# One output product of the mixing stage issued inside the attention units, and the down products' wait on block sums issued later

## Chip, cores, metric

The kernel runs on one core of one Trainium2 chip. The metric is the device time of one execution in microseconds (us). All data is fp32.

## The reference

The reference is two blocks over 256 tokens of width 1024. The first has a retention group, an RWKV group and sixteen experts. The second has two layers of mixing and feed-forward, and the change lies there:

```
for layer in range(DEPTH_2):                       # 2 layers
    h = rmsnorm(x, norm_mix[layer])
    z = h @ w_in[layer]
    ...
    o_a = nsa_mixer(...)      # 4 heads: compressed, selected and window attention, gated
    o_b = diff_mixer(...)     # 4 heads, difference of two softmaxes
    o_c = mlstm_mixer(...)    # 4 heads
    o_d = dilated_mixer(...)  # 4 heads
    x = x + jnp.concatenate([o_a, o_b, o_c, o_d], axis=-1) @ w_out[layer]
    h = rmsnorm(x, norm_ffn[layer])
    x = x + (jax.nn.silu(h @ w_gate[layer]) * (h @ w_up[layer])) @ w_down[layer]
return rmsnorm(x, norm_final)
```

## The kernel before, in words

TensorE (PE), ScalarE (ACT), VectorE (DVE) and the DMA queue on SyncE (SP) each run one straight program written out by hand. Semaphores order them: an instruction with waits holds everything behind it on its engine. Weights of 2 MB per slot stream through a ring in SBUF, in a fixed order; `W.take` waits for the landing of the next slot, and a count on `W.used` lets SP load the slot that has been left. PSUM has eight banks of 128 x 512 fp32.

**Mixing** (function `mixing`). Tokens lie in two tiles `t` of 128. The width 1024 of the concatenated mixers falls into four groups `g` of 256: 0 is `o_a`, 1 `o_b`, 2 `o_c`, 3 `o_d`. The attention runs as `NU` = 14 units `u`, one mixer part and token tile each; the last are 10 and 11 (mlstm), 12 and 13 (dilated, token tile 0 and 1). For each unit PE does

- `score(u + 1)` (dilated units: L2268) into banks 0 and 1,
- `turn(u)` (L2282), transposes of the probabilities into banks 2 and 3, which waits for DVE's `weigh(u)` (for the dilated units L2536) and so for ACT's exponentials (L2386),
- projection work and other items that fill the gaps (`fills`, `halved`); at the last two units nothing is left,
- `values(u)` (L2303) into bank 4 or 5, which waits for ACT's copy of the transposes (`keep`, L2404).

The item `o0` (L2231) transposes group 0 of the attention output at the end of unit 11. It is kept to `mixT` by ACT (L2373). Items such as `o0` take bank 6 or 7, in turns worked out in `banks`; `held` says whose copy must be over first.

After the units PE takes the two weight slots of `w_out` and runs, in this order: `o3`, `out_product(0, 0)`, `out_product(0, 1)`, `out_product(3, 0)`, `o1`, `o2`, `out_product(3, 1)`, and the four products of groups 1 and 2. `out_product(g, t)` (L2334) is four matmuls of 512 columns, 128 x 128 weights, which the profile shows as eight records, two each. Banks 0 and 1 collect token tile 0, banks 2 and 3 token tile 1. `o3` waits for DVE's output of unit 13 (L2559). `o1` and `o2` wait for `o_ready`: that is the end of a chain of norms on DVE (L2653 to L2671) with one square root on ACT (L2454). On ACT the copies of `o3`, `o1` and `o2` are queued behind that square root. Then DVE adds the banks to `x` (L2678), and the feed-forward begins with its norm.

**Feed-forward** (function `feed_forward`). The products use a seven-product scheme (Strassen's, in Winograd's form) for 2 x 2 blocks; the weight-side sums are made by DVE (`block_sum`, L2936, four per weight slot, counted on `sums_ready`). Twelve units of gate and up (L2750) are followed by the down product (L2821): for each `j` from 0 to 7, products `m1` to `m7`, one matmul (two records) each. `m1` to `m3` read the weights as they landed, `m4` to `m7` read block sums. At each even `j`:

```
w = W.take(pe)
pe.wait_ge(sums_ready, 4 * (UNITS + j // 2) + 4)
```

so all seven wait until the fourth block sum of the slot is made. At `j` = 0, `m1` also waits for the gates (ACT, L2876) and `m4` for DVE's last copy out of the units (L2974). The last three `j` are run product by product, behind a wait for all block sums (L2846).

Of the kernel before, what the change touches and what calls it, by code (L numbers as in the profile page):

```python
# [12 lines left out]
P = 128  # L13
# [2011 lines left out]
def mixing(nc, K, layer):  # L2025

    A, W = K.A, K.W
# [55 lines left out]
    by = lambda name: "dve" if name in turns or name in ("f", "qk0", "qk1") else "act"  # L2083
    ordinal = [sum(by(other) == by(name) for other in items[:n + 1]) for n, name in enumerate(items)]
    banks, held, turn_of = [], [], {6: -1, 7: -1}
    for n, name in enumerate(items):
        mine = (6, 7) if name[:2] == "qk" else ((6,) if turn_of[6] <= turn_of[7] else (7,))
        banks.append(mine)
        held.append([turn_of[b] for b in mine if turn_of[b] >= 0])
        for b in mine:  # L2090
            turn_of[b] = n

    keys = lambda u: 16 if units[u][0] == "cmp" else P * (units[u][1] + 1)
    maps = lambda u: 2 if units[u][0] == "diff" else 4
    scale = {"cmp": HD ** -0.5, "slc": HD ** -0.5, "win": HD ** -0.5, "dil": HD ** -0.5, "diff": 32 ** -0.5}
# [39 lines left out]
    def tensor(pe):  # L2135
# [150 lines left out]
        def values(u):  # L2286
# [16 lines left out]
                    last = nc.tensor.matmul(out, probsT[:, u % 2, (t + 1) * j + k, :], v, start=(k == 0), stop=(k == t))  # L2303
            last.then_inc(pv_made, 1)

        turn_input(0, 1)
        pe.wait_ge(t_scaled, 1)
        pe.wait_ge(t_kept, 1)
# [4 lines left out]
        for u in range(NU):  # L2313
            if u + 1 < NU:
                score(u + 1)
            if u in leads:
                item(leads[u])
            if u in halved:
                half_job(halved[u], 0)
            turn(u)  # L2320
            if u in halved:
                half_job(halved[u], 1)
            for name in fills[u]:
                item(name)
            values(u)
        ws = [W.take(pe) for _ in range(2)]
        pe.wait_ge(scores_kept, NU)
        pe.wait_ge(pt_kept, NU)

        def out_product(g, t):  # L2330
            kept(f"o{g}")
            for k in range(2 * g, 2 * g + 2):
                for n in range(2):
                    last = nc.tensor.matmul(K.ps[:, 2 * t + n, :], K.mixT[:, k, P * t:P * t + P], ws[n][:, k, :],  # L2334
                                            start=(g == 0 and k == 0), stop=(g == 2 and k == 5))
                    if g == 0 and t == 0 and k == 0 and n == 0:
                        last.then_inc(W.used, 1)
            if g == 2:
                last.then_inc(out_made, 1)

        item("o3")
        out_product(0, 0)
        out_product(0, 1)
        out_product(3, 0)
        item("o1")
# [112 lines left out]
    def vector(dve, meanwhile):  # L2458
# [216 lines left out]
        meanwhile(dve)  # L2675
        for t in range(TT):
            dve.wait_ge(out_made, t + 1)
            nc.vector.tensor_tensor(K.x[:, t, :], K.x[:, t, :], K.ps[:, 2 * t:2 * t + 2, :].rearrange("p a b -> p (a b)"),  # L2678
                                    ALU.add).then_inc(x_ready, 1)

    A.high = top
# [3 lines left out]
def feed_forward(nc, K, layer):  # L2685
# [49 lines left out]
    def tensor(pe):  # L2735
# [91 lines left out]
        for j in range(TAIL):  # L2827
            if j % 2 == 0:
                w = W.take(pe)
                pe.wait_ge(sums_ready, 4 * (UNITS + j // 2) + 4)  # L2830
            if j == 0:
                pe.wait_ge(gate_opened, FCH)
                pe.wait_ge(took, 5 * (UNITS - 1))
            for n in range(1, 8):
                if j == 0 and n == 4:
                    pe.wait_ge(hid_opened, FCH)
                    pe.wait_ge(took, 5 * UNITS)
                if j % 2 == 0 and n == 3:
                    pe.wait_ge(hid_summed, FCH * layer + j // 2 + 1)
                last = down(j, f"m{n}", w)  # L2840
                if j % 2 == 0 and n == 1:
                    last.then_inc(W.used, 1)
                elif j % 2 == 1 and n == 7:
                    last.then_inc(made, 1)
# [453 lines left out]
```

## Time and profile before

| | |
|---|---|
| median of 3 runs | 2016.33 us (2011.97 to 2017.17) |
| the profiled execution, its own time | 2017.03 us |
| its span in the trace | 2015.2 us |
| PE busy | 1690.9 us, 84% |
| DVE busy | 700.5 us, 35% |
| ACT busy | 355.9 us, 18% |
| mean granted TensorE clock | 0.909 of full speed |
| load of a 2 MB slot of `w_out`, issue to landing | 7.7 us |

Time outside the span is 1.8 us. "Idle before" is the time in which an engine had nothing running ahead of an instruction, with the instruction whose end let it go. A row of the timeline merges instructions of one line. PEclk (clock) is the share of full speed granted to TensorE: 1.00 is 2.4 GHz, 0.50 is 1.2 GHz. The first mixing layer of the second block spans about 1163 to 1361 us, the first feed-forward layer 1363 to 1585, the second mixing layer 1585 to 1784, the second feed-forward layer the rest.

### The profile page before, as it was taken

The page shows a single profiled execution, that of the slowest core. Times are in us where ns is not written, and L with a number is a line of the kernel's source. Part 1 is how long each engine was busy: PE and PEld are TensorE (multiplying, and loading weights), DVE is VectorE, ACT ScalarE, POOL GpSimd, SP SyncE. Part 2 cuts the span into 40 slices and gives each one's busy share as a digit, 9 for nine tenths or more (in the row PEclk, how much of TensorE's full clock was granted, in tenths as well). Part 3 has the DMA queues.
Part 4 walks back from the last instruction along what each step waited for, and adds up shares of the span by engine and source line. Part 5 has one row for each costly group of instructions (what it writes and reads, how often), then busy time and mean ns, then how long its engine had stood idle before and what let it go on. Part 6 is the DMA issues. An engine that isn't in the chain of part 4 may idle for free.

```text
span 2015.2 us, 31978 instructions
## 1 busy us (share of the span) xinstructions
PE 1690.9 (84%) x14184; PEld 1151.5 (57%) x14184; DVE 700.5 (35%) x1247; ACT 355.9 (18%) x827; POOL 91.0 (5%) x94
## 2 busy tenths in 40 slices
PE   6999898987989675655655689988999999899997
PEld 3665458957975431211211257758994476669963
DVE  2005373363332300000000124555664244536663
ACT  2010122342231220000000122421010124310000
POOL 0000003402311000000000000000000000000000
PEclk9999898987999788877877889989999899899999
DMA  9521111040024599999999952214454522225440
GB/s 373 198 90 78 67 42 44 4 168 2 4 73 162 209 406 428 427 428 427 429 427 428 428 187 84 84 42 171 170 204 167 217 88 84 84 84 209 168 178 21
DMA packets 35593, 382.08 MB, mean 190 GB/s; under 512 B 6977, under 2 KB 10433, under 8 KB 12673
## 3 DMA queue, kind: packets, MB, share of 16 engines
q1 hardware_dynamic: 35458, 380.04, 47.2%
q8 instruction: 113, 1.85, 0.4%
q14 instruction: 22, 0.18, 0.0%
HBM read 378.98 MB, written 1.05 MB: 189 GB/s over the span
## 4 chain that ended last, share of the span: by engine, by line
PE 50%; DMA 11%; DVE 3%; ACT 1%; issue 1%; SPq 0%; DVEq 0%; ACTq 0%
PE psum L2750 14%; PE psum L1873 7%; PE psum L2821 7%; DMA arena<-in_w_moe 6%; PE psum L2162 6%; DMA weight_ring<-in_w_moe 5%; PE psum L2165 3%; PE psum L2334 3%; PE psum L1848 3%; PE psum L2303 1%; PE psum L1828 1%; PE psum L2282 1%; PE psum L2268 1%; PE psum L2191 1%; PE psum L1898 0%
## 5 line engine op out<-in xcount | busy, mean ns | idle before, releaser
L1873 PE MATMUL psum<-weight_ring,arena 128*32 128x512 f32 x640 | 142.6, 721 | 127.7 <-DMA arena<-in_w_moe 93.5
L1269 PE MATMUL psum<-arena 64*64 64x64 f32 x4608 | 150.8, 223 | 19.6 <-PEq L962 8.8
L2750 PE MATMUL psum<-arena 128*128 128x128 f32 x1408 | 165.2, 275 | 1.7 <-DVE arena L2953 1.7
L2750 PEld LDWEIGHTS psum<-arena 128*128 128x128 f32 x1408 | 161.1, 192 | 2.0 <-issue 2.0
L1269 PEld LDWEIGHTS psum<-arena 64*64 64x64 f32 x4608 | 143.2, 138 | 27.0 <-issue 22.8
L1873 PEld LDWEIGHTS psum<-weight_ring,arena 128*32 128x32 f32 x640 | 36.1, 130 | 205.3 <-issue 205.3
L2002 DVE COPY arena<-psum 128x512 f32<-128x512 f32 x16 | 11.1, 692 | 371.3 <-PE psum L1873 371.3
L2750 PE MATMUL psum<-arena,weight_ring 128*128 128x128 f32 x1056 | 131.8, 283 | 4.7 <-ACT arena L2867 2.6
L1873 PE MATMUL psum<-arena 128*32 128x512 f32 x384 | 107.0, 718 | 33.5 <-DMA weight_ring<-in_w_moe 33.1
L2750 PEld LDWEIGHTS psum<-arena,weight_ring 128*128 128x128 f32 x1056 | 127.2, 199 | 5.9 <-DVE arena L2998 3.1
L2162 PE MATMUL psum<-arena,weight_ring 128*128 128x256 f32 x512 | 124.2, 396 | 0.0
L2162 PEld LDWEIGHTS psum<-arena,weight_ring 128*128 128x128 f32 x512 | 98.6, 197 | 19.7 <-issue 4.1
L2936 DVE TENSOR_TENSOR arena<-weight_ring 128x1024 f32<-128x1024 f32 (+1 forms) x72 | 81.3, 1129 | 55.4 <-PE psum L2821 55.2
L1453 DVE TENSOR_TENSOR arena<-arena,psum 128x512 f32<-128x512 f32 (+1 forms) x80 | 50.7, 633 | 86.0 <-PE psum L1269 85.1
L2165 PE MATMUL psum<-weight_ring,arena 128*128 128x512 f32 (+1 forms) x192 | 77.6, 554 | 2.6 <-issue 1.3
L2821 PE MATMUL psum<-arena 128*128 128x512 f32 x176 | 78.5, 592 | 0.0
L2821 PE MATMUL psum<-weight_ring,arena 128*128 128x512 f32 x132 | 63.2, 619 | 9.7 <-DVE arena L2936 6.0
L434 PE MATMUL psum<-arena,weight_ring 128*128 128x256 f32 x288 | 65.6, 391 | 2.8 <-PEq L198 2.8
L1923 ACT ACTIVATE arena<-psum 128x256 f32<-128x256 f32 x16 | 6.2, 384 | 348.2 <-PE psum L1883 348.2
L434 PEld LDWEIGHTS psum<-arena,weight_ring 128*128 128x128 f32 x288 | 56.4, 197 | 11.3 <-issue 3.3
L1848 PE MATMUL psum<-arena 128*128 128x512 f32 x128 | 59.3, 605 | 1.2 <-ACT arena L1938 1.2
L2334 PE MATMUL psum<-weight_ring,arena 128*128 128x512 f32 x128 | 59.1, 622 | 0.0
(497 smaller groups left out, 2244.0 us busy)
## 6 DMA issues: line engine op xcount, KB each, us to landing
weight_ring<-in_w_moe SPq DMA_DIRECT2D x60, 2048.0 KB, 20.2
arena<-in_w_moe SPq DMA_DIRECT2D x36, 2048.0 KB, 20.4
weight_ring<-in_w_in SPq DMA_DIRECT2D x23, 2048.0 KB, 8.1
weight_ring<-in_w_mod SPq DMA_DIRECT2D x12, 2048.0 KB, 8.0
weight_ring<-in_w_gate SPq DMA_DIRECT2D x12, 2048.0 KB, 7.6
weight_ring<-in_w_up SPq DMA_DIRECT2D x12, 2048.0 KB, 7.6
weight_ring<-in_w_down SPq DMA_DIRECT2D x12, 2048.0 KB, 7.6
weight_ring<-in_w_out SPq DMA_DIRECT2D x6, 2048.0 KB, 7.7
```

What stands on the lines that cost most here:

```text
L434: last = nc.tensor.matmul(bank[:, 0:T], w[:, k, P * b:P * b + P], hT[:, k, T:2 * T], start=(k == 0), stop=(k == KT - 1))
L1269: last = nc.tensor.matmul(K.ps[half[d], bank, column + HD * n:column + HD * n + HD], lhs(d, h), rhs(d, h), start=True, stop=True, skip_gro ...
L1453: done = nc.vector.tensor_tensor(inv[:, par, 0:kinds, which, :], inv[:, par, 0:kinds, which, :], src, ALU.add)
L1828: last = nc.tensor.matmul(K.ps[:, d % 4, 0:256], K.h2[:, t, P * d:P * d + P], sel[:, t, cols], start=(t == 0), stop=(t == 1))
L1848: last = nc.tensor.matmul(K.ps[:, 2 * t + n, :], scatter_to[:, e, P * t:P * t + P], parts[:, n, :], start=(e == 0), stop=(e == NE - 1))
L1873: last = nc.tensor.matmul(K.ps[strip(j), 4, :], xsT[:, k, CAP * e:CAP * e + CAP], ws[j][:, k, :], start=(k == 0), stop=(k == KT - 1), skip ...
L2162: last = nc.tensor.matmul(K.ps[:, bank, 0:T], w[:, k, P * b:P * b + P], hT[:, k, :], start=(k == 0), stop=(k == KT - 1))
L2165: last = nc.tensor.matmul(K.ps[:, bank, 0:width], hT[:, k, P * b:P * b + P], w[:, k, 0:width], start=(k == 0), stop=(k == KT - 1))
L2334: last = nc.tensor.matmul(K.ps[:, 2 * t + n, :], K.mixT[:, k, P * t:P * t + P], ws[n][:, k, :], start=(g == 0 and k == 0), stop=(g == 2 an ...
L2750: last = nc.tensor.matmul(K.ps[:, bank, P * n:P * n + P], lhs, rhs, start=(n == 0 and k == 0 and name in ("m1", "m5", "m6")), stop=(k == 3 ...
L2821: return nc.tensor.matmul(K.ps[:, int(name[1]) - 1, :], lhs, rhs, start=(j == 0), stop=(j == NFT // 2 - 1), skip_group_check=True)
L2936: nc.vector.tensor_tensor(out, x, y, op).then_inc(sums_ready, 1)
```

## The change

1. `out_product(0, 0)` moves from behind `o3` to unit 12, between that unit's `turn` and `values`. The two `W.take` for `w_out` move with it. It first waits for the copies of the items that last held banks 6 and 7 (`late_takers`). Token tile 0 is now collected in banks 6 and 7 instead of 0 and 1; tile 1 stays in 2 and 3; `o3`, `o1` and `o2` take banks 0, 1 and 0. The `W.used` count of its first matmul moves too.
2. In the down product the wait on `sums_ready` moves from `m1` to `m4` at each even `j` below 8.

```diff
+    late = {"o3": 0, "o1": 1, "o2": 0}
     for n, name in enumerate(items):
+        if name in late:
+            banks.append((late[name],))
+            held.append([at["o3"]] if name == "o2" else [])
+            continue
...
+    late_takers = sorted(set(turn_of.values()))
...
+        ws = []
+        out_bank = lambda t, n: 6 + n if t == 0 else 2 + n
...
+                    last = nc.tensor.matmul(K.ps[:, out_bank(t, n), :], K.mixT[:, k, P * t:P * t + P], ws[n][:, k, :],
...
             for name in fills[u]:
                 item(name)
+            if u == 12:
+                ws.extend(W.take(pe) for _ in range(2))
+                for m in late_takers:
+                    pe.wait_ge(took[by(items[m])], ordinal[m])
+                out_product(0, 0)
             values(u)
-        ws = [W.take(pe) for _ in range(2)]
...
         item("o3")
-        out_product(0, 0)
         out_product(0, 1)
...
-            nc.vector.tensor_tensor(K.x[:, t, :], K.x[:, t, :], K.ps[:, 2 * t:2 * t + 2, :].rearrange("p a b -> p (a b)"),
+            nc.vector.tensor_tensor(K.x[:, t, :], K.x[:, t, :], K.ps[:, 6 - 4 * t:8 - 4 * t, :].rearrange("p a b -> p (a b)"),
...
             if j % 2 == 0:
                 w = W.take(pe)
-                pe.wait_ge(sums_ready, 4 * (UNITS + j // 2) + 4)
...
+                if j % 2 == 0 and n == 4:
+                    pe.wait_ge(sums_ready, 4 * (UNITS + j // 2) + 4)
                 last = down(j, f"m{n}", w)
```

PE at the end of the first mixing layer, from `values(12)` on, before. The names in brackets are the semaphores that the instruction waits on; `stage9_act_took` and `stage9_dve_took` count copies out of PSUM by ACT and DVE, `weights_landed` the landing of weight slots.

```order
L2303 MATMUL psum<-arena 128x64 [waits stage9_act_took,stage9_o_taken,stage9_pt_kept]
L2303 MATMUL psum<-arena 128x64 x3
L2282 MATMUL psum<-arena 128x128 [waits stage9_pt_kept,stage9_p_ready]
L2282 MATMUL psum<-arena 128x128 x7
L2303 MATMUL psum<-arena 128x64 [waits stage9_act_took,stage9_o_taken,stage9_pt_kept]
L2303 MATMUL psum<-arena 128x64 x7
L2231 MATMUL psum<-arena 128x128 [waits stage9_pt_kept,stage9_dve_took,stage9_scores_kept,stage9_o_taken,weights_landed_1,weights_landed_0]
L2231 MATMUL psum<-arena 128x128 x3
L2334 MATMUL psum<-weight_ring,arena 128x512 [waits stage9_act_took]
L2334 MATMUL psum<-weight_ring,arena 128x512 x3
L2334 MATMUL psum<-weight_ring,arena 128x512 [waits stage9_act_took]
L2334 MATMUL psum<-weight_ring,arena 128x512 x3
```

The same place in the changed program, from the moved product on (the line numbers there are 6 higher for L2282, L2303 and L2231, and the product is L2319):

```order
L2319 MATMUL psum<-weight_ring,arena 128x512 [waits stage9_act_took,stage9_dve_took,weights_landed_1,weights_landed_0]
L2319 MATMUL psum<-weight_ring,arena 128x512 x3
L2309 MATMUL psum<-arena 128x64 [waits stage9_act_took,stage9_o_taken,stage9_pt_kept]
L2309 MATMUL psum<-arena 128x64 x3
L2288 MATMUL psum<-arena 128x128 [waits stage9_pt_kept,stage9_p_ready]
L2288 MATMUL psum<-arena 128x128 x7
L2309 MATMUL psum<-arena 128x64 [waits stage9_act_took,stage9_o_taken,stage9_pt_kept]
L2309 MATMUL psum<-arena 128x64 x7
L2237 MATMUL psum<-arena 128x128 [waits stage9_o_taken,stage9_pt_kept,stage9_scores_kept]
L2237 MATMUL psum<-arena 128x128 x3
L2319 MATMUL psum<-weight_ring,arena 128x512 [waits stage9_act_took]
L2319 MATMUL psum<-weight_ring,arena 128x512 x3
```

The four matmuls of the product stand ahead of `values(12)` instead of behind `o3`, and the waits for the landed weights went with them.

PE in the first feed-forward layer, at `j` = 0 and `j` = 1 of the down product and the begin of `j` = 2, before:

```order
L2821 MATMUL psum<-weight_ring,arena 128x512 [waits stage10_gate_opened,stage10_took,stage10_block_sums_ready,weights_landed_4]
L2821 MATMUL psum<-weight_ring,arena 128x512
L2821 MATMUL psum<-weight_ring,arena 128x512 [waits layers_hid_summed]
L2821 MATMUL psum<-arena 128x512 [waits stage10_took,stage10_hid_opened]
L2821 MATMUL psum<-arena 128x512 x3
L2821 MATMUL psum<-weight_ring,arena 128x512 x3
L2821 MATMUL psum<-arena 128x512 x4
L2821 MATMUL psum<-weight_ring,arena 128x512 [waits stage10_block_sums_ready,weights_landed_0]
L2821 MATMUL psum<-weight_ring,arena 128x512
L2821 MATMUL psum<-weight_ring,arena 128x512 [waits layers_hid_summed]
L2821 MATMUL psum<-arena 128x512 x4
```

The same place in the changed program (L2821 is L2832 there):

```order
L2832 MATMUL psum<-weight_ring,arena 128x512 [waits stage10_took,stage10_gate_opened,weights_landed_4]
L2832 MATMUL psum<-weight_ring,arena 128x512
L2832 MATMUL psum<-weight_ring,arena 128x512 [waits layers_hid_summed]
L2832 MATMUL psum<-arena 128x512 [waits stage10_block_sums_ready,stage10_took,stage10_hid_opened]
L2832 MATMUL psum<-arena 128x512 x3
L2832 MATMUL psum<-weight_ring,arena 128x512 x3
L2832 MATMUL psum<-arena 128x512 x4
L2832 MATMUL psum<-weight_ring,arena 128x512 [waits weights_landed_0]
L2832 MATMUL psum<-weight_ring,arena 128x512
L2832 MATMUL psum<-weight_ring,arena 128x512 [waits layers_hid_summed]
L2832 MATMUL psum<-arena 128x512 [waits stage10_block_sums_ready]
```

The wait on `stage10_block_sums_ready` went from the first matmul of an even `j` to the fourth; `stage10_took` and `stage10_hid_opened` at the fourth stay.

## Rows read from the trace of the kernel before

**Rows 1.** The page, part 4: chain that ended last, by engine

```profile
PE 50%; DMA 11%; DVE 3%; ACT 1%; issue 1%; SPq 0%; DVEq 0%; ACTq 0%
```

**Rows 2.** Timeline of PE, first layer: start, length in us, line, records, idle before

```profile
1315.06 2.00 PE L2303 MATMUL psum<-arena 128*128 128x64 f32 x16 [0.74 <-ACT arena L2404]
...
1318.06 0.66 PE L2282 MATMUL psum<-arena 128*128 128x128 f32 x4
1319.41 1.10 PE L2303 MATMUL psum<-arena 128*128 128x64 f32 x8 [0.69 <-ACT arena L2404]
1323.16 1.16 PE L2282 MATMUL psum<-arena 128*128 128x128 f32 x8 [2.65 <-DVE arena L2536]
1325.50 3.68 PE L2303 MATMUL psum<-arena 128*128 128x64 f32 x16 [1.18 <-ACT arena L2404]
1329.85 1.09 PE L2231 MATMUL psum<-arena 128*128 128x128 f32 x4 [0.68 <-DVE arena L2559]
1330.73 12.24 PE L2334 MATMUL psum<-weight_ring,arena 128*128 128x512 f32 x24
1342.81 1.04 PE L2231 MATMUL psum<-arena 128*128 128x128 f32 x8
1343.68 17.33 PE L2334 MATMUL psum<-weight_ring,arena 128*128 128x512 f32 x40
```

**Rows 3.** Timeline of ACT and DVE, same stretch

```profile
1316.43 0.58 ACT L2373 ACTIVATE arena<-psum 128x512 f32<-128x512 f32 x1
...
1329.28 0.42 DVE L2559 TENSOR_TENSOR arena<-psum,arena 128x256 f32<-128x256 f32 x1 [5.51 <-PE psum L2303]
...
1334.54 0.58 ACT L2373 ACTIVATE arena<-psum 128x512 f32<-128x512 f32 x1
...
1338.00 0.43 DVE L2671 TENSOR_TENSOR arena<-arena 128x256 f32<-128x256 f32 x1
```

**Rows 4.** Windows, first layer: length, busy (records) of PE, PEld, DVE, ACT, POOL, PEclk

```profile
1324.00:1326.00 2.00, 0.82 (x6) 0.52 (x4) 0.00 (x0) 1.63 (x3) 0.00 (x0) 0.51 0.03 8
```

**Rows 5.** Timeline of PE and ACT, second mixing layer

```profile
1745.74 1.97 PE L2282 MATMUL psum<-arena 128*128 128x128 f32 x8 [2.65 <-DVE arena L2536]
...
1748.89 3.68 PE L2303 MATMUL psum<-arena 128*128 128x64 f32 x16 [1.18 <-ACT arena L2404]
...
1757.93 0.58 ACT L2373 ACTIVATE arena<-psum 128x512 f32<-128x512 f32 x1
...
1766.13 1.04 PE L2231 MATMUL psum<-arena 128*128 128x128 f32 x8
```

**Rows 6.** Timeline of PE, first mixing layer, a short gap

```profile
1262.25 0.92 PE L2268 MATMUL psum<-arena 64*128 64x128 f32 x8 [1.24 <-DVE arena L2471]
1263.11 3.42 PE L2162 MATMUL psum<-arena,weight_ring 128*128 128x256 f32 x8
```

**Rows 7.** Timeline of PE and DVE, first feed-forward layer, start of the down product

```profile
1509.10 1.06 PE L2750 MATMUL psum<-arena 128*128 128x128 f32 x8
...
1510.71 1.22 DVE L2936 TENSOR_TENSOR arena<-arena,weight_ring 128x1024 f32<-128x1024 f32 x1
1511.85 0.28 DVE L2974 TENSOR_TENSOR arena<-psum,arena 128x128 f32<-128x128 f32 x1
...
1512.03 2.81 PE L2821 MATMUL psum<-weight_ring,arena 128*128 128x512 f32 x6 [1.88 <-issue]
```

**Rows 8.** Timeline of PE, second feed-forward layer, the same place

```profile
1935.32 2.81 PE L2821 MATMUL psum<-weight_ring,arena 128*128 128x512 f32 x6 [1.87 <-issue]
```

**Rows 9.** Timeline of PE, first feed-forward layer, end of the down product

```profile
1563.33 4.34 PE L2821 MATMUL psum<-weight_ring,arena 128*128 128x512 f32 x6 [2.99 <-DVE arena L2936]
```

**Rows 10.** Timeline of SP: issues of weight loads, first mixing layer

```profile
1220.28 22.86 SPq L118 DMA_DIRECT2D weight_ring<-in_w_out  x2
...
1332.68 0.33 SPq L118 DMA_DIRECT2D weight_ring<-in_w_gate  x1
```

**Rows 11.** The page, part 6: issues of w_out slots, count, KB, us to landing

```profile
weight_ring<-in_w_out SPq DMA_DIRECT2D x6, 2048.0 KB, 7.7
```

More of the change, by code:

```diff
@@ L2304, in values, with out_product @@
             last.then_inc(pv_made, 1)
+        ws = []
+        out_bank = lambda t, n: 6 + n if t == 0 else 2 + n
+        def out_product(g, t):
+            kept(f"o{g}")
+            for k in range(2 * g, 2 * g + 2):
+                for n in range(2):
+                    last = nc.tensor.matmul(K.ps[:, out_bank(t, n), :], K.mixT[:, k, P * t:P * t + P], ws[n][:, k, :],
+                                            start=(g == 0 and k == 0), stop=(g == 2 and k == 5))
+                    if g == 0 and t == 0 and k == 0 and n == 0:
+                        last.then_inc(W.used, 1)
+            if g == 2:
+                last.then_inc(out_made, 1)
         turn_input(0, 1)
@@ L2324, in tensor @@
                 item(name)
+            if u == 12:
[3 more added lines that the diff above has]
+                out_product(0, 0)
             values(u)
-        ws = [W.take(pe) for _ in range(2)]
         pe.wait_ge(scores_kept, NU)
         pe.wait_ge(pt_kept, NU)
[L2330 to L2339, printed above, removed]
         item("o3")
-        out_product(0, 0)
         out_product(0, 1)
```

## The prediction

> **What bounds the kernel now.** I read the chain that ended last first: PE holds 50% of it, the other engines 3% or less, DMA 11% [rows 1], and the DMA part lies in the experts, ahead of everything the change touches. In the second block the end is set by PE: whatever it idles, and whatever it runs at half clock, is time. Then I read the timeline of PE around the two edits, in both layers, and beside it ACT and DVE, to see who lets each PE instruction go.
>
> At the end of the attention the timeline shows PE short of work. `turn(12)` ends at 1318.72 and `values(12)` starts only at 1319.41; before `turn(13)` 2.65 us are idle, waiting for DVE; before `values(13)` 1.18, before `o3` 0.68 [rows 2]. In this stretch the granted clock falls to 0.51 [rows 4]: the sixteen records of `values(13)` take 3.68 us where unit 11's sixteen took 2.00, `o3`'s four take 1.09, and the 24 records of three output products 12.24, where forty later ones take 17.33, 0.433 each [rows 2]. Behind `o3` PE is busy without a gap up to `o1` at 1342.81 and on through the forty records. `o1` waits for the DVE chain whose last step ends at 1338.00 + 0.43 = 1338.43 [rows 3], so PE comes 4.4 us later than it could: here PE is the bound, not DVE.
>
> At the start of the down product PE idles 1.88 us [rows 7] and 1.87 in the second layer [rows 8]. The timeline calls it "issue", but DVE's fourth block sum runs from 1510.71 to 1511.93, and PE starts at 1512.03: that is the wait.
>
> **The moved product, first layer.** It adds no work. Eight records leave the busy stretch behind `o3` and go into the hole before `values(12)`.
>
> What it waits for is there. `o0` is copied at 1316.43 + 0.58 = 1317.01 [rows 3]. The banks 6 and 7 were last held by `o0` and by `qk1`, which is older. The two `w_out` slots were issued by 1220.28 + 22.86 = 1243.14 [rows 10]; with 7.7 us to land [rows 11] they are in SBUF by 1251. So it starts at 1318.72 and takes 8 x 0.433 = 3.46 us, to 1322.2. `values(12)` is queued behind it and with 1.10 us ends at 1323.3. `turn(13)` was let go by DVE at 1323.16 anyway, so it is late by 0.1. DVE's output of unit 12 comes behind the same DVE step, and ACT's copies for unit 13 depend on `turn(13)` alone: nobody else waits for `values(12)`.
>
> If the clock holds, `turn(13)` saves 0.07 and `values(13)` 3.68 - 2.00 = 1.68. DVE's L2559 and all of its chain come 1.68 + 0.07 - 0.1 = 1.65 us earlier: `o3`'s copy ends at 1334.54 + 0.58 - 1.65 = 1333.5 [rows 3], the chain at 1336.8. PE starts `o3` at 1328.2 and `out_product(0, 1)` at 1328.7, through at 1332.2. Now something is late that was hidden: `out_product(3, 0)` needs the copy of `o3`, which ACT makes behind its square root. It waits 1.4 us, runs from 1333.6 to 1337.1, and `o1` follows at once, 0.3 us behind the DVE chain. That is 1342.81 - 1337.1 = 5.7 us.
>
> The unknown is the clock. The stretch still has a gap of 1.18 and one of 0.6 around the sixteen narrow records of `values(13)`, and the new 1.4. What such gaps do, the rows show both ways: the 0.69 left the clock up, but behind a gap of 1.24 eight records took 3.42 us, 0.43 each for 256 columns, which is half speed [rows 6]. If one slow spell begins behind `values(13)`, `o3` and six records of `out_product(0, 1)` cost twice: 0.5 + 6 x 0.43 = 3.1 us, less the 1.4 of waiting that covers it, and some start already inside it; I put it at 1.4 lost, which leaves 4.3. If the clock falls before `values(13)` as it did, the DVE chain doesn't move, and only the product's own 3.4 is gained: sixteen records behind `o3` instead of 24, `o1` at 1339.4, still behind the chain's 1338.43. The bounds are 3.4 and 5.7. I take 5.0, midway between whole and one spell, since the longest gap is now 1.4 instead of 2.65.
>
> **The second layer** repeats the rows, but there `turn(13)` was slow too, 1.97 instead of 1.09 [rows 5]. With the clock held the chain moves by 0.88 + 1.68 - 0.1 = 2.46 us. `o3`'s copy ends at 1757.93 + 0.58 - 2.46 = 1756.05, `out_product(3, 0)` at 1759.6, and `o1` comes at 1759.6 instead of 1766.13: 6.5. With one spell 5.1; bounds 3.4 and 6.5; I take 5.8.
>
> **What moves with it.** The `W.used` count of the product's first matmul lets SP issue the next `w_gate` load at about 1318.8 instead of 1332.68 [rows 10]. That slot serves the third feed-forward unit, 50 us later; no transfer is in the way, none depends on it sooner: nothing. The banks in other places, and DVE's adds out of them, have the same sizes and the same order: nothing. The order behind `o1` is unchanged, so what `o1` gains reaches the end of the stage, and the next stage starts on DVE's add, which waits for PE.
>
> **The wait in the down product.** At `j` = 0, `m1` to `m3` (six records, 2.6 us) can start where the unit's last product lets go, at 1510.15, instead of 1512.03. They end at 1512.75. `m4` then wants the block sum, ready at 1511.93, and DVE's L2974, which ends at 1511.85 + 0.28 = 1512.13 [rows 7]. Both are over by then, with 0.6 to spare. So the whole 1.88 goes, and 1.87 in the second layer. It can't be more than 2.0, and is nothing if another of `m1`'s waits were the last; I take 1.85 each, 3.7. At `j` = 2, 4 and 6 the timeline has no gap: nothing, and even 1.9 us sooner the sums are there. The 2.99 before the last three `j` [rows 9] is a chain from PE to DVE and back, and its wait isn't touched: it moves along and stays, with its slow records (4.34 for six).
>
> **Sum.** 5.0 + 5.8 + 3.7 = 14.5 us. Against the profiled execution's own 2017.03 that gives 2002.5. The median of the runs is 0.7 lower, so I predict 2016.33 - 14.5 = 2001.8. About 0.3%, 6 us, is what a measurement of this kernel can tell from no change.
>
> **The rivals.**
>
> *The clock never falls in the stretch.* 5.7 + 6.5 + 3.7 = 15.9, so 2000.4. For it: the longest gap shrinks from 2.65 to 1.4. Against it: the fall behind 1.24 [rows 6]. The Trainium skill (TensorE: Matmul & The Clock Gate, "Why this matters for your kernels") blames long idle gaps alone for a clock that drops mid-kernel, and by that rule this rival would be sure. The trace doesn't agree with it, as the fall behind 1.24 us of idle shows.
>
> *The clock falls before `values(13)` all the same.* Then 3.4 + 3.4 + 3.7 = 10.5, so 2005.8. For it: in the second layer the clock was down already at `turn(13)` [rows 5]. Against it: 3.46 us of wide records now stand in that hole.
>
> *The down products don't start sooner.* If the gap marked "issue" [rows 7, 8] isn't the block sum, only 5.0 + 5.8 = 10.8 remain, 2005.5. The agreement of 1511.93 and 1512.03, and the 0.6 us to spare, speak against it.
>
> *The gain is eaten by other clock falls.* All later stages move against the clock's own course. Each start behind a stall costs what the six records show: 4.34 - 6 x 0.433 = 1.7 us [rows 9]. Five such places hit more than before would take 8.5 and leave 6: 2010.3, no change that can be told. But the second layer sits elsewhere in time than the first and has the same stalls with the same lengths, so the places are as likely to gain.
>
> *Slower: the product holds the queue of unit 12.* It stands ahead of `values(12)` and `turn(13)`, and carries the waits for weights, banks and `o0`. If it starts late by D, the clock is down and the DVE chain moves out by D: `o1` comes at 1338.43 + D. From D = 4.4 us on the layer is slower than before; with the down products' gain, D = 9.3 is needed for a loss of over 0.3%. With D = 12: 2016.33 + 2 x 7.6 - 3.7 = 2027.8. The waits ended 1.7 us (`o0`) and 67 us (weights) earlier, so little speaks for it.
>
> **How the numbers follow.** Forecast 0.45 (its own range 1998.5 to 2004.5), clock never falls 0.19, clock falls first 0.17, down products alone missing 0.08, eaten elsewhere 0.08, slower 0.03. The first four are faster by over 0.3%: 0.89; the same 0.08; slower 0.03. The range holds the first four cases: from 2000.4 less 2 us for the scatter of the runs, 1998.4, to 2005.8 plus 2, 2007.8. The 0.11 outside are the last two.
>
> **What the changed profile should show.** Eight records of L2319 starting near 0.1 us behind `turn(12)`, 3.5 us long, in both layers; `turn(13)` let go by DVE, at most 0.2 late; `values(13)` in about 2.0 us instead of 3.68; a new idle of up to 1.5 before `out_product(3, 0)`, whose releaser is ACT's L2373; `o1` 4 to 6.5 us sooner after `turn(12)` than the 24.1 of before. In the down product no gap before `m1`, none before `m4`. I am wrong if `values(13)` is still at 3.68, if PE waits for DVE at `o1` by more than 1 us, if the product waits for `weights_landed`, or if the gap at `m1` comes back before `m4`.

## The result, and the profile after

The changed kernel takes 1997.03 us, the median of six runs (1990.59 to 2007.04). The kernel before took 2016.53, also of six. The ratio is 0.991, with a 95% interval of 0.9892 to 0.9928: 14.5 to 21.8 us less. I had forecast 2001.8, 14.5 us less, with a range down to 1998.4. The direction was right, the size too small, and the result lies 1.4 us below the range. One execution behind this document, of the changed kernel padded by 0.43 us (below), took 4275 us; it is left out of the medians and ratios, and nothing here explains it.

The page of the changed kernel: span, busy time of the engines, and the chain by engine.

```profile
span 1992.1 us, 31970 instructions
...
PE 1677.0 (84%) x14184; PEld 1141.1 (57%) x14184; DVE 700.0 (35%) x1247; ACT 356.0 (18%) x827; POOL 91.0 (5%) x94
...
PE 50%; DMA 11%; DVE 3%; ACT 1%; issue 1%; SPq 0%; DVEq 0%; ACTq 0%
```

PE still holds 50% of the chain, as in [rows 1]. What changed is the length of the span, 1992.1 us instead of 2015.2; the profiled execution's own time is 1994.0.

The timeline of PE, first mixing layer of the changed kernel, to be read against [rows 2] (L2288 was L2282, L2309 L2303, L2237 L2231, and L2319 is the output product):

```profile
1312.72 0.66 PE L2288 MATMUL psum<-arena 128*128 128x128 f32 x4
1313.21 3.60 PE L2319 MATMUL psum<-weight_ring,arena 128*128 128x512 f32 x8
1316.65 1.00 PE L2309 MATMUL psum<-arena 128*128 128x64 f32 x8
1317.82 1.09 PE L2288 MATMUL psum<-arena 128*128 128x128 f32 x8 [0.17 <-DVE arena L2547]
1320.09 2.00 PE L2309 MATMUL psum<-arena 128*128 128x64 f32 x16 [1.18 <-ACT arena L2415]
1322.76 1.09 PE L2237 MATMUL psum<-arena 128*128 128x128 f32 x4 [0.68 <-DVE arena L2570]
1323.64 8.14 PE L2319 MATMUL psum<-weight_ring,arena 128*128 128x512 f32 x16
1331.62 1.04 PE L2237 MATMUL psum<-arena 128*128 128x128 f32 x8
1332.49 17.33 PE L2319 MATMUL psum<-weight_ring,arena 128*128 128x512 f32 x40
```

The product's eight records start at 1313.21, directly behind `turn(12)`, and take 3.6 us. `turn(13)` is let go by DVE after 0.17 us of idle instead of 2.65. `values(13)` takes 2.00 instead of 3.68. From `turn(12)` to `o1` it is 1331.62 - 1312.72 = 18.90 us instead of 24.75: 5.85 less.

ACT's copy of `o3` and the last step of the DVE chain, same kernel, against [rows 3]:

```profile
1327.45 0.58 ACT L2384 ACTIVATE arena<-psum 128x512 f32<-128x512 f32 x1
...
1330.91 0.43 DVE L2682 TENSOR_TENSOR arena<-arena 128x256 f32<-128x256 f32 x1
```

The copy ends at 1328.03. The sixteen records of 8.14 us are `out_product(0, 1)` and `out_product(3, 0)`. The eighth starts at 1327.60 and the ninth, which needs the copy, at 1328.08: that is 0.48 us instead of the usual 0.43, so of the new wait only 0.05 us is left. The last eight run to 1331.5, and `o1` starts 0.3 us behind the DVE chain's 1331.34.

The second mixing layer, against [rows 5]:

```profile
1731.02 1.09 PE L2288 MATMUL psum<-arena 128*128 128x128 f32 x8 [0.17 <-DVE arena L2547]
1733.29 2.01 PE L2309 MATMUL psum<-arena 128*128 128x64 f32 x16 [1.18 <-ACT arena L2415]
1735.97 1.09 PE L2237 MATMUL psum<-arena 128*128 128x128 f32 x4 [0.68 <-DVE arena L2570]
1736.85 9.58 PE L2319 MATMUL psum<-weight_ring,arena 128*128 128x512 f32 x16
1746.27 1.04 PE L2237 MATMUL psum<-arena 128*128 128x128 f32 x8
```

Here `turn(12)` stands at 1725.92, so the stretch is 20.35 us instead of 25.49: 5.14 less. The sixteen records take 9.58, 1.4 more than in the first layer. ACT's copy of `o3` ends at 1741.24 here, 1.6 us before the ninth record wants it, so there is no wait for it at all. The windows show why (length, busy us of PE, PEld, DVE, ACT, POOL with records, then the granted clock):

```profile
1320.00:1322.00 2.00, 1.91 (x16) 1.86 (x16) 0.00 (x0) 1.31 (x2) 0.00 (x0) 1.00 0.38 156
1322.00:1324.00 2.00, 1.32 (x6) 1.25 (x6) 1.64 (x6) 0.00 (x0) 0.00 (x0) 0.53 0.01 4
1324.00:1326.00 2.00, 2.00 (x4) 0.75 (x3) 1.90 (x4) 0.00 (x0) 0.00 (x0) 0.61 0.00 0
...
1738.00:1740.00 2.00, 2.00 (x3) 0.72 (x3) 1.90 (x4) 0.00 (x0) 0.00 (x0) 0.50 0.00 0
```

In both layers `values(13)` now runs at full clock (2.00 and 2.01 us). The clock falls behind it, at `o3`, to about 0.5 (1.2 GHz), for what is called a slow spell from here on. In the first layer it makes `o3`'s four records and the next two slow, and the time lost is time that PE would otherwise have waited for `o3`'s copy. In the second layer `o3` and the next six are slow, and 1.4 us of it shows.

The start of the down product, against [rows 7]:

```profile
1498.63 2.74 PE L2832 MATMUL psum<-weight_ring,arena 128*128 128x512 f32 x6
...
1499.36 1.22 DVE L2948 TENSOR_TENSOR arena<-arena,weight_ring 128x1024 f32<-128x1024 f32 x1
...
1500.49 0.28 DVE L2986 TENSOR_TENSOR arena<-psum,arena 128x128 f32<-128x128 f32 x1
...
1501.21 3.60 PE L2832 MATMUL psum<-arena 128*128 128x512 f32 x8
```

`m1` follows the last eight records of the units (L2761, start 1497.74) after 0.89 us from start to start; before it was 1512.03 - 1509.10 = 2.93. So 2.04 us are gone, and the same in the second layer (1912.20 - 1911.31). `m4` starts without a gap, 0.4 us behind DVE's L2986.

So the edit's own stretches give 5.85 + 5.14 + 2 x 2.04 = 15.1 us. The spans differ by 23.1. The experiments ask where the other 8 come from and how much of them is the change's.

### The profile page after: what moved, and what is told of

The parts are those of the page before. It is cut to its first block, busy times and chain, and to the rows that moved or that the text cites. A ratio compares the mean times of both kernels' runs of the same rounds, so it can differ in the third digit from the quotient of the medians.

```text
span 1992.1 us, 31970 instructions
## 1 busy us (share of the span) xinstructions
PE 1677.0 (84%) x14184; PEld 1141.1 (57%) x14184; DVE 700.0 (35%) x1247; ACT 356.0 (18%) x827; POOL 91.0 (5%) x94
## 3 DMA queue, kind: packets, MB, share of 16 engines
q8 instruction: 113, 1.85, 0.4%
## 4 chain that ended last, share of the span: by engine, by line
PE 50%; DMA 11%; DVE 3%; ACT 1%; issue 1%; SPq 0%; DVEq 0%; ACTq 0%
PE psum L2761 14%; PE psum L1873 7%; PE psum L2832 7%; DMA arena<-in_w_moe 7%; PE psum L2168 6%; DMA weight_ring<-in_w_moe 5%; PE psum L2171 3%; PE psum L1848 3%; PE psum L2319 3%; PE psum L2309 1%; PE psum L1828 1%; PE psum L2288 1%; PE psum L2274 1%; PE psum L2197 1%; PE psum L2251 0%
## 5 line engine op out<-in xcount | busy, mean ns | idle before, releaser
L2761 PE MATMUL psum<-arena 128*128 128x128 f32 x1408 | 165.2, 275 | 1.7 <-DVE arena L2965 1.7
L2761 PEld LDWEIGHTS psum<-arena 128*128 128x128 f32 x1408 | 161.1, 192 | 2.0 <-issue 2.0
L2761 PE MATMUL psum<-arena,weight_ring 128*128 128x128 f32 x1056 | 129.8, 280 | 4.7 <-ACT arena L2879 2.6
L2761 PEld LDWEIGHTS psum<-arena,weight_ring 128*128 128x128 f32 x1056 | 125.2, 196 | 6.0 <-DVE arena L2969 2.8
L2832 PE MATMUL psum<-arena 128*128 128x512 f32 x176 | 78.5, 592 | 0.0
L2832 PE MATMUL psum<-weight_ring,arena 128*128 128x512 f32 x132 | 63.5, 621 | 6.0 <-DVE arena L2948 6.0
L2319 PE MATMUL psum<-weight_ring,arena 128*128 128x512 f32 x128 | 59.6, 623 | 0.0
```

Source lines behind the costliest of these rows:

```text
L2319: last = nc.tensor.matmul(K.ps[:, out_bank(t, n), :], K.mixT[:, k, P * t:P * t + P], ws[n][:, k, :], start=(g == 0 and k == 0), stop=(g == ...
L2761: last = nc.tensor.matmul(K.ps[:, bank, P * n:P * n + P], lhs, rhs, start=(n == 0 and k == 0 and name in ("m1", "m5", "m6")), stop=(k == 3 ...
L2832: return nc.tensor.matmul(K.ps[:, int(name[1]) - 1, :], lhs, rhs, start=(j == 0), stop=(j == NFT // 2 - 1), skip_group_check=True)
```

## The experiments

Each kernel was timed beside the kernel before on the same chip, 4 to 12 executions of it, in three batches; a ratio is to the kernel before of the same batch. One execution of each was profiled. From each profile I took the starts of the same PE instructions, and list here the differences, in us: one execution per line. "Start-up" ends where the second stage's first matmul starts. "To 12" ends at `turn(12)` of the first mixing layer, "out 0" and "out 1" run from `turn(12)` to `o1`, "ff 0" and "ff 1" from `o1` to the first down matmul, "down 0" to the first matmul of the second mixing layer, "mix 1" to its `turn(12)`, "down 1" to the end. The last column is the sum from "out 0" on: everything the change can reach.

| kernel | start-up | to 12 | out 0 | ff 0 | down 0 | mix 1 | out 1 | ff 1 | down 1 | from 12 |
|---|---|---|---|---|---|---|---|---|---|---|
| before | 48.8 | 1269.2 | 24.7 | 169.2 | 73.2 | 155.4 | 25.5 | 169.2 | 79.8 | 697.1 |
| before again | 43.9 | 1273.1 | 24.8 | 169.2 | 73.2 | 155.4 | 25.5 | 169.2 | 79.8 | 697.0 |
| changed | 43.6 | 1269.1 | 18.9 | 167.0 | 73.3 | 154.0 | 20.4 | 165.9 | 79.9 | 679.4 |
| changed again | 44.0 | 1269.6 | 18.9 | 167.0 | 73.3 | 154.0 | 20.4 | 166.0 | 79.9 | 679.5 |
| product alone | 43.9 | 1268.9 | 18.9 | 169.0 | 71.7 | 152.3 | 19.1 | 169.1 | 79.8 | 680.0 |
| wait alone | 43.8 | 1269.0 | 24.7 | 167.2 | 71.6 | 152.1 | 25.5 | 167.2 | 78.2 | 686.6 |
| product twice | 44.2 | 1269.7 | 22.2 | 169.0 | 71.7 | 154.0 | 23.8 | 167.8 | 78.3 | 686.8 |
| before, padded | 48.6 | 1269.1 | 24.8 | 170.3 | 71.7 | 152.2 | 25.6 | 169.2 | 79.8 | 693.7 |
| changed, padded | 44.1 | 1273.1 | 18.9 | 167.4 | 73.3 | 152.4 | 19.1 | 167.1 | 78.2 | 676.5 |
| changed, padded more | 44.1 | 1273.2 | 20.4 | 167.0 | 74.7 | 150.6 | 18.9 | 167.0 | 79.9 | 678.6 |
| tighter | 48.7 | 1269.4 | 21.7 | 164.1 | 73.3 | 154.0 | 21.7 | 164.1 | 79.9 | 678.8 |
| spares in the tail | 48.8 | 1273.5 | 20.4 | 165.9 | 71.4 | 155.0 | 18.9 | 167.0 | 78.1 | 676.7 |
| spares in the stalls | 50.1 | 1269.5 | 18.9 | 164.6 | 71.4 | 150.7 | 19.0 | 164.6 | 78.1 | 667.2 |

In the last kernel the spares ahead of the second mixing layer count to "down 0". In "tighter" `o1` comes behind one more product, so its "out" and "ff" count together.

**The kernel before, again.** No edit.

> The kernel before, unchanged, once more. Theory 'two stretches': the change is worth what its own stretches show, 11.0 us at the output products and 4.1 us at the down products, and the rest of the 19.5 us between the medians is scatter of stages that it doesn't touch (in the two profiled executions 5.3 us lie ahead of unit 12, all of it in the first 50 us). Then this run is at ratio 1.000 within 0.003, and the start of the last attention units in its profile may differ by several us from the 1318.1 of before. Rival 'all of it is real': the start of unit 12 is again near 1318 us and the scatter is below 2 us.

Ratio 0.9998 (0.9985 to 1.0012). The theory of two stretches expected scatter ahead of unit 12, and it is there, in two places that the change doesn't touch: the start-up takes about 44 or about 49 us, and the way from there to unit 12 1269 or 1273. The two nearly cancel here, so that unit 12 starts at 1317.0, near the 1318.1 of before, with 4.9 us less in one piece and 3.8 more in the other. From unit 12 on the two executions agree within 0.1 us in every piece. That neither theory had said.

**The changed kernel, again.** No edit.

> The changed kernel, unchanged, once more. Two stretches: ratio 0.9925 (2016.5 less 15.1), from unit 12's turn to o1 again 18.9 to 20.4 us in each layer, no gap before the down product's m1; what lies ahead of unit 12 starts anywhere within some 5 us. All of it is real: ratio 0.9903 (less 19.5) and unit 12 again at about 1312.7.

1996.93 us, ratio 0.9907 (0.9888 to 0.9925). "All of it is real" had 0.9903, "two stretches" 0.9925, and the interval holds both, the second at its edge. The pieces decide: they show 697.1 - 679.4 = 17.7 us, and again repeat within 0.1. That is 2.6 us more than the 15.1 of the edit's own stretches, and less than the 19.5. So 17.7 is the change's, by two profiles of each kernel, and most of the 5.3 us ahead of unit 12 was a start-up of 48.8 in the one profile of before.

**The moved product alone.**

```diff
             if j % 2 == 0:
                 w = W.take(pe)
+                pe.wait_ge(sums_ready, 4 * (UNITS + j // 2) + 4)
...
-                if j % 2 == 0 and n == 4:
-                    pe.wait_ge(sums_ready, 4 * (UNITS + j // 2) + 4)
```

> The moved product alone; the down product's wait as before. Two stretches: 11 us less than before, ratio 0.9945, the stretch from unit 12's turn to o1 19 to 20.5 us instead of 24.75 and 25.5, the gap of 1.88 before m1 still there. All of it is real: 15 us less, ratio 0.9925.

1995.96 us, ratio 0.9907 (0.9891 to 0.9923): as fast as the whole change, where "two stretches" had 0.9945. Against the changed kernel "out 0" is the same 18.9. The feed-forward layers are longer: "ff 0" by the 2.0 that the wait costs, "ff 1" by 3.2. But "down 0", "mix 1" and "out 1" are shorter, by 1.6, 1.6 and 1.3 us. The stall before the last three `j` of the first down product is the same length as in [rows 9], and the six records behind it are not slow:

```profile
1552.08 2.81 PE L2832 MATMUL psum<-weight_ring,arena 128*128 128x512 f32 x6 [2.99 <-DVE arena L2947]
```

**The moved wait alone.**

```diff
             if j % 2 == 0:
                 w = W.take(pe)
-                pe.wait_ge(sums_ready, 4 * (UNITS + j // 2) + 4)
...
+                if j % 2 == 0 and n == 4:
+                    pe.wait_ge(sums_ready, 4 * (UNITS + j // 2) + 4)
```

> The moved wait alone; the output product as before. Two stretches: 4.1 us less than before, ratio 0.998, gap before m1 gone in both layers, values(13) again at 3.68 us. All of it is real: 4 to 8 us less, 0.996 to 0.998. A third theory, that the wait at m1 costs nothing on the path: 1.000.

2006.63 us, ratio 0.9954 (0.9937 to 0.9971), more than twice my 4.1 us. "Ff 0" and "ff 1" give the 2.0 each; the other 6.4 of the 10.5 come in "down 0", "mix 1" and "down 1". The parts alone give 17.1 and 10.5 by the pieces, together 17.7: they don't add. Put on top of the moved product, the moved wait brought only 0.6 us, although its 4.1 us are gone from their own places.

**The product in both places.** The edit is against the changed kernel. The spare product of unit 12 has the same waits, banks and matmuls; its result is overwritten. The wait in the down product is back at `m1` (not shown).

```diff
-                out_product(0, 0)
+                spare_product()
...
         item("o3")
+        out_product(0, 0)
         out_product(0, 1)
```

> The first product runs in unit 12 as a spare (its result isn't used) and again behind o3 as before; the down product's wait as before. So unit 12's hole is filled, but nothing leaves the busy stretch. Theory 'half of the gain is the clock': values(13) takes 2.0 us, the DVE chain comes 1.65 to 2.5 us sooner, and from unit 12's turn to o1 it is 22.5 to 23.5 us in the first layer and 24 to 25 in the second, against 24.75 and 25.49 of before: faster by 2 to 3 us there, though PE does 6.9 us more work. Rival 'the gain is only the eight records that left': the stretch is as long as before or longer, 24.7 to 28 us.

Here PE does 6.9 us more work than before, and the kernel is faster: 2001.91 us, ratio 0.994 (0.992 to 0.996). The timeline of PE (L2325 is the product behind `o3`):

```profile
1321.31 2.00 PE L2309 MATMUL psum<-arena 128*128 128x64 f32 x16 [1.18 <-ACT arena L2422]
1323.99 1.09 PE L2237 MATMUL psum<-arena 128*128 128x128 f32 x4 [0.68 <-DVE arena L2577]
1324.87 11.40 PE L2325 MATMUL psum<-weight_ring,arena 128*128 128x512 f32 x24
1336.11 1.04 PE L2237 MATMUL psum<-arena 128*128 128x128 f32 x8
```

`values(13)` is at 2.00, and the stretch to `o1` is 22.17 us, 2.6 less than before; in the second layer it is 23.78, 1.7 less, with `values(13)` at 2.28. Both are 0.2 to 0.3 us below what I had expected, and far from the rival's 24.7 to 28. So of the 11.0 us at the output products 4.3 come from the clock that stays up and the DVE chain that starts sooner. The other 6.7, about 3.4 a layer, are by difference those of the eight records that left. The rest of the gain of this kernel, 5.9 of 10.2 us from unit 12 on, lies in stages that the edit doesn't touch ("down 0", "mix 1", "ff 1", "down 1").

**The kernel before, padded.** Two spare matmuls, 1.1 us, in the first feed-forward layer.

```diff
         for u in range(UNITS):
+            if layer == 0 and u == 4:
+                nc.tensor.matmul(K.ps[:, 7, 0:512], hT[:, 0, 0:P], hT[:, 0:2, 0:256], start=True, stop=True)
+                nc.tensor.matmul(K.ps[:, 7, 0:128], hT[:, 0, 0:P], hT[:, 0:1, 0:128], start=True, stop=True)
             unit(u, ws[u] if u < 2 else W.take(pe))
```

> The kernel before with two spare matmuls (512 and 128 columns, four records, 1.1 us, result not used) in front of the fifth feed-forward unit of the first layer. Theory 'where a stall meets the clock's course decides': in the two executions of before the slow spells fall in the same places from the first mixing layer on, so they are not chance but repeat; 1.1 us later, the stall before the last three j of the first down product misses its slow spell (six records 2.7 us instead of 4.3) and the next mixing layer starts better, so down0 to mix1 takes about 71.6 us instead of 73.2 and the stretch behind it 152 to 153 instead of 155.4: in all 3 to 4 us faster than before with 1.1 us more work, ratio 0.998. Rival 'the clock's falls average out': slower by 1.1 us, 1.0005, stretches unchanged.

Ratio 0.998 (0.9968 to 0.9992), 2012.53 us: faster with more work, as the theory of the clock's course had it, and outside the rival's 1.0005. "Ff 0" grows by 1.1, "down 0" shrinks by 1.5 and "mix 1" by 3.2. The row behind the stall:

```profile
1563.99 2.81 PE L2821 MATMUL psum<-weight_ring,arena 128*128 128x512 f32 x6 [3.01 <-DVE arena L2939]
```

It is 2.81 us for the six records instead of 4.34 [rows 9], behind a stall of 3.01.

**The changed kernel, padded**, by one matmul of 256 columns and by the two above.

```diff
+            if layer == 0 and u == 4:
+                nc.tensor.matmul(K.ps[:, 7, 0:256], hT[:, 0, 0:P], hT[:, 0:1, 0:256], start=True, stop=True)
```

> The changed kernel with one spare matmul of 256 columns (two records, 0.43 us, result not used) at the same place. Clock's course decides: the stall in the first down product misses its slow spell (71.7 us instead of 73.3), and what the later stretches do is open within 3 us, in a way that repeats. Averages out: 0.4 us slower than the changed kernel.

> The changed kernel with the pad of the padded kernel before (512 and 128 columns, 1.1 us) instead of 256 columns. Position theory: a different pad gives a different, repeating set of slow spells, within 3 us of the changed kernel either way; if the pad's gain was chance, it is 1.1 us slower than the changed kernel.

With 0.43 us: 1991.93 us, ratio 0.9883 (0.9865 to 0.99). Where I had expected the gain, in "down 0", nothing moved (73.3): a miss. It came in "mix 1", "out 1" and "down 1" instead, and "ff 1" got 1.2 longer. With 1.1 us: 1999.11, ratio 0.991 (0.9895 to 0.9925). That is no better than the changed kernel, and the interval is too wide to tell "position" from "1.1 us slower". Its profile already differs in "out 0", ahead of the pad, by 1.5 us, as that of the spares in the tail does: the spell behind `values(13)` lasts twice as long there. So the repetition isn't complete. Both executions had the 1273 to unit 12, but so had the kernel padded by 0.43 us, whose "out 0" is 18.9. What decides it is open.

**Tighter.**

```diff
+        out_product(0, 1, (0,))
         item("o3")
-        out_product(0, 1)
+        out_product(0, 1, (1,))
         out_product(3, 0)
+        out_product(3, 1)
         item("o1")
         item("o2")
-        out_product(3, 1)
```

The third argument of `out_product` is new: it names which half of the product to run. In ACT's program `item("o3")` goes ahead of the wait for `ss_ready`.

> The changed kernel with half of out_product(0, 1) before o3 and half behind, o3's copy taken by ACT ahead of its square root, and out_product(3, 1) ahead of o1. The new gap before out_product(3, 0) and the 0.68 before o3 are filled. From turn(12) to the end of the output products 1.9 us less in the first layer and 1.9 to 3.3 in the second (39.8 and 41.2 us in the changed kernel). Two stretches: 4 us less than the changed kernel, ratio to before 0.989; clock's course decides: the same in these stretches, but the total may be off that by 3 us either way.

1994.87 us, ratio 0.9895 (0.9872 to 0.9918). From `turn(12)` to the end of the output products it got 0.1 us shorter in the first layer instead of 1.9 (37.1 to 37.0), and 1.6 in the second (38.6 to 37.0). "Out" and "ff" together are 185.8 in both, against 185.9 and 186.3: in the second layer the feed-forward's first group took 5.83 us instead of 5.31 and gave part of it back.

```profile
1325.51 2.00 PE L2309 MATMUL psum<-arena 128*128 128x64 f32 x16 [1.18 <-ACT arena L2416]
1327.35 3.57 PE L2319 MATMUL psum<-weight_ring,arena 128*128 128x512 f32 x4
1330.71 0.71 PE L2237 MATMUL psum<-arena 128*128 128x128 f32 x4
1331.26 8.75 PE L2319 MATMUL psum<-weight_ring,arena 128*128 128x512 f32 x20
1339.84 1.04 PE L2237 MATMUL psum<-arena 128*128 128x128 f32 x8
1341.13 14.00 PE L2319 MATMUL psum<-weight_ring,arena 128*128 128x512 f32 x32 [0.25 <-ACT arena L2385]
```

The 0.68 before `o3` is gone, and a new 0.25 has come behind `o2`, for ACT's copy of `o1`. But four records of `out_product(0, 1)` at 1327.35 take 3.57 us, 0.85 each from start to start: the slow spell behind `values(13)` now costs its full time. In the changed kernel's first layer there was nothing left to gain from the earlier copy, since slow records had filled all but 0.05 us of that wait.

**Spares in the stalls.** First in the tail of the down products alone (shown), then also at the start of the feed-forward layers (11 and 4 matmuls of 128 columns, behind an added wait for `x`) and of the second mixing layer (8 and 4).

```diff
         ws = [W.take(pe) for _ in range(2)]
+        for _ in range(3):
+            nc.tensor.matmul(K.ps[:, 7, :], hidT[:, 0, 0, :], hidT[:, 0, 0:4, :], start=True, stop=True)
         pe.wait_ge(sums_ready, 4 * (UNITS + FCH))
```

> The changed kernel with three spare matmuls of 512 columns (six records, 2.6 us, result not used, bank 7) in the stall of 2.99 us before the last three j of both down products. Theory 'a slow spell comes from the hole in PE's work at its place': the six records behind the stall take 2.7 to 2.9 us instead of 4.5 in both layers, 1.6 us less each, 3.3 in all less than the changed kernel if nothing else moves, with up to 3 us either way from the later stalls after the first layer's. Rival 'the spell comes whatever PE does': 4.5 stays, same time as the changed kernel.

> The same, and spare 128-column matmuls in the stalls at the start of both feed-forward layers (11 before the transposes, 4 behind) and of the second mixing layer (8 and 4). Hole theory: the first L2761 group of 32 takes 3.7 us instead of 5.3 to 5.8, and the first L2171 group of 8 takes 3.5 instead of 5.4; 2.1 + 1.6 + 1.9 + 3.3 = about 9 us less than the changed kernel, so 1988. Rival: not faster, or slower by the spares that outlast their stall (up to 1 us).

Tail alone: 1992.11 us, ratio 0.9876 (0.9859 to 0.9892). The spares and the six records behind them:

```profile
1556.69 2.74 PE L2859 MATMUL psum<-arena 128*128 128x512 f32 x6
1559.63 2.84 PE L2832 MATMUL psum<-weight_ring,arena 128*128 128x512 f32 x6 [0.21 <-DVE arena L2950]
```

It is 2.84 us for the six records instead of 4.51, and each tail is 1.9 us shorter ("down 0" 71.4, "down 1" 78.1); "mix 1" is 1.0 longer, and the whole from unit 12 on 2.7 less than the changed kernel, where I had expected 3.3. All stalls: 1985.9 us, ratio 0.9852 (0.9828 to 0.9877), against 0.9907 for the changed kernel in another batch; the pieces say 679.4 - 667.2 = 12.2 us, where I had expected 9. At the start of the first feed-forward layer:

```profile
1357.06 2.69 PE L2786 MATMUL psum<-arena 128*128 128x128 f32 x22 [0.30 <-PE psum L2319]
1359.59 1.04 PE L2779 MATMUL psum<-arena 128*128 128x128 f32 x8
1360.47 1.06 PE L2789 MATMUL psum<-arena 128*128 128x128 f32 x8
1361.95 3.81 PE L2767 MATMUL psum<-arena,weight_ring 128*128 128x128 f32 x32 [0.43 <-ACT arena L2892]
```

The 32 records take 3.81 us, where the changed kernel takes 5.81. This is the fastest version here: it beats both kernels by doing more work on PE. The waits that the spares fill are as long as before within 0.2 us; what got shorter are the records in and behind them (the transposes between the spares, L2779, take 1.04 us instead of 1.64).

## Why the prediction was right and wrong

**The moved product: right in its steps, with luck in the sum.** The product starts at once, `turn(13)` is late by at most 0.2, `values(13)` takes 2.00, and in the first layer `o1` comes 0.3 us behind the DVE chain, as I had worked out. I took 5.0 and 5.8 us, and it is 5.85 and 5.14: 11.0 against 10.8. The luck is that the two layers miss by 0.85 and 0.66 in opposite directions, and 5.85 is above my bound of 5.7. The one spell that I had put in half came in both layers, at `o3`. In the first it cost nothing, since it filled the new wait for `o3`'s copy, of which 0.05 us was left; in the second it cost 1.4, as priced. The new idle of up to 1.5 us is in neither.

**The down product's wait: right in its place.** 2.04 in each layer against 1.85; I had named 2.0 as the most. (Of these 4.1 us only 0.6 remain as the difference between the product alone and the whole change, by what else moved.) "Issue" in [rows 7, 8] was the block sum.

**Everything else at nothing: the step that failed.** I wrote that all later stages "move against the clock's own course" but "the places are as likely to gain", and so put zero into the sum and no width into the range. That term, zero in the sum, measured 2.6 us: 1.4 in the second mixing layer, 1.2 at the start of the second feed-forward layer, 0.2 at the first, less 0.2 in the tails. The slow first groups behind the stalls show it; before:

```profile
1363.71 1.06 PE L2762 MATMUL psum<-arena 128*128 128x128 f32 x8 [2.69 <-DVE arena L2994]
1366.09 6.55 PE L2750 MATMUL psum<-arena,weight_ring 128*128 128x128 f32 x32 [1.32 <-ACT arena L2867]
...
1587.63 6.69 PE L2165 MATMUL psum<-weight_ring,arena 128*128 128x512 f32 x8 [1.28 <-DVE arena L2610]
...
1789.42 6.52 PE L2750 MATMUL psum<-arena,weight_ring 128*128 128x128 f32 x32 [1.32 <-ACT arena L2867]
```

and changed:

```profile
1352.52 1.64 PE L2773 MATMUL psum<-arena 128*128 128x128 f32 x8 [2.69 <-DVE arena L3006]
1355.48 5.81 PE L2761 MATMUL psum<-arena,weight_ring 128*128 128x128 f32 x32 [1.32 <-ACT arena L2879]
...
1549.85 4.51 PE L2832 MATMUL psum<-weight_ring,arena 128*128 128x512 f32 x6 [2.99 <-DVE arena L2948]
...
1574.32 5.37 PE L2171 MATMUL psum<-weight_ring,arena 128*128 128x512 f32 x8 [1.28 <-DVE arena L2621]
...
1769.55 5.31 PE L2761 MATMUL psum<-arena,weight_ring 128*128 128x128 f32 x32 [1.32 <-ACT arena L2879]
```

It is 5.37 instead of 6.69 in the second mixing layer, 5.31 instead of 6.52 in the second feed-forward layer, and in the tail 4.51 instead of 4.34. In the first feed-forward layer 5.81 stands against 6.55, but the transposes ahead take 1.64 instead of 1.06, so that only 0.2 is gained: the spell came sooner. The mistake was to take the falls of the clock as chance with a mean of zero. From unit 12 on they repeat: before twice, and changed twice, agree piece by piece within 0.1 us. A shift of the program picks another set of spells. The padded kernel before shows that this is cause and not company: 1.1 us of spare work took 4.5 us out of stages that weren't edited.

The sum of it: 15.1 + 2.6 = 17.7 us, by 3.2 more than forecast. That alone would have been 2016.33 - 17.7 = 1998.6, just inside the range. The rest, to the 19.5 between the medians of six, is scatter ahead of unit 12, for which the range had no room left: the start-up takes about 44 or 49 to 50 us and the way to unit 12 1269 or 1273, by execution, whatever the kernel. In later batches before had medians of 2014.89, 2016.91 and 2016.46.

Both levels go with the clock. In the four executions with 1273, TensorE was at 1.2 GHz for 306 us of the way to unit 12, in the nine others for 296 to 299. In the start-up the PE rows show it, before and before again:

```profile
29.13 5.97 PE L259 MATMUL psum<-arena 128*128 128x128 f32 x32
```

```profile
27.47 3.17 PE L259 MATMUL psum<-arena 128*128 128x128 f32 x24
30.81 1.09 PE L259 MATMUL psum<-arena 128*128 128x128 f32 x8 [0.17 <-DVE arena L345]
```

The same 32 records take 5.97 us or 3.17 + 1.09. All five executions with a start-up of 48.6 us or more have them slow, the eight with 44 have them fast. What decides the level was not tried. Open, too, is which places a given shift hits: for the changed kernel with 0.43 us I named the wrong one.

**The rivals.** "The clock never falls in the stretch" didn't come true: it fell behind `values(13)`, and the longest gap ahead of it in the stretch is 1.18 us. "The clock falls before `values(13)`" is answered by its 2.00 us, "the down products don't start sooner" by the 2.04, and "slower" by the product's start directly behind `turn(12)`. The Trainium skill (TensorE: Matmul & The Clock Gate, "Why this matters for your kernels") blames long gaps alone. The runs agree that filling a gap can keep the clock (2.84 instead of 4.51), but the same stall of 2.99 us has a slow spell behind it in before and none in the product alone, so the gap's length alone isn't what decides. "Eaten by other clock falls" was the right mechanism with the wrong sign.

## What to carry to other kernels

Look first for a hole in the bounding engine just ahead of a place where that engine is late, and ask what ready work can fill it: it gives its own time (3.4 us a layer here) and, on TensorE, can keep the clock up behind it. Before calling the clock's falls noise, profile the same kernel twice: where they repeat they belong to the version. What an edit is worth is then open by what the falls elsewhere do until it is run; here that was 2.6 us for the whole change and 6.4 for the moved wait alone. Where no real work fits into a stall, spare matmuls may pay: 12.2 us here.

## What the runs showed that I had not expected

- The clock's slow spells repeat from one execution to the next over 700 us, although the start-up differs by 5 us: 697.1 and 697.0 for before, 679.4 and 679.5 for changed. The Trainium skill (TensorE: Matmul & The Clock Gate, "What's actually happening") says that the number of slow matmuls at a kernel's start varies from run to run. The runs agree for the start-up (44 or 49 us). Later the falls keep to the program: in all thirteen profiles the first one behind the start-up comes 162.2 to 163.2 us after the second stage's first matmul. Why they do is open.
- Two edits that each save time by themselves, 17.1 and 10.5 us, save 17.7 together.
- Work that computes nothing made kernels faster: before by 0.2% (1.1 us added), changed from 0.9907 to 0.9852 of before.
- A wait and a slow spell in one place can cost no more than one of them: closing the waits ("tighter") gained 0.1 us in the first layer where 1.9 were expected, and 1.6 in the second.
